# An SSD mixer in a two-block network: the state's share of the second chunk summed by TensorE, and the step sizes worked out earlier

## What is computed

```python
def mamba2_mixer(h, w_in, conv_w, conv_b, dt_bias, a_log, d_skip, norm_g, w_out):
    proj = h @ w_in                         # z (2048), xbc (3072), dt_raw (32)
    xbc = jax.nn.silu(causal_dwconv(xbc, conv_w, conv_b))
    dt = jax.nn.softplus((dt_raw + dt_bias).astype(jnp.float32))
    a = -jnp.exp(a_log.astype(jnp.float32))
    y = ssd_chunked(xs, dt, a, bm, cm) + xs * d_skip[:, None]
    yz = (y * jax.nn.silu(z))               # then an RMS norm in 4 groups, times norm_g
    return y @ w_out

def ssd_chunked(xs, dt, a, bm, cm):
    a_cs = jnp.cumsum(da, axis=-1)
    xdt = x * dtc[..., None]
    decay = jnp.exp(jnp.where(causal, a_cs[..., :, None] - a_cs[..., None, :], -jnp.inf))
    cb = jnp.einsum('bclgn,bcsgn->bcgls', cc, bc)
    y_diag = jnp.einsum('bcgrls,bcsgrp->bclgrp', cb[:, :, :, None] * decay, xdt)
    decay_states = jnp.exp(a_cs[..., -1:] - a_cs)
    states = jnp.einsum('bclgn,bcgrl,bclgrp->bcgrpn', bc, decay_states, xdt)
    y_off = jnp.einsum('bclgn,bcgrpn,bcgrl->bclgrp', cc, prev, jnp.exp(a_cs))
    return (y_diag + y_off)
```

## Times and profile before

| | |
|---|---|
| median of 3 runs | 1482.74 us (1481.03 to 1485.03) |
| the profiled execution | 1484.64 us |
| its span, first to last instruction | 1482.9 us |
| PE / PEld busy | 93% / 89% of the span |
| DVE / ACT / POOL busy | 70% / 51% / 10% |
| mean granted TensorE clock | 0.964 of 2.4 GHz |

### The profile page before, as it was taken

The page is one execution under the profiler, slowest core; times in us unless marked ns, Lnnn a source line. Parts: engine busy times, 40 slices in busy tenths (PEclk is TensorE's granted clock), DMA queues, the critical chain, the costliest instruction groups (busy, mean ns, idle before and its releaser), DMA issues.

```text
span 1482.9 us, 30231 instructions
## 1 busy us (share of the span) xinstructions
PE 1381.3 (93%) x12445; PEld 1325.4 (89%) x12445; DVE 1040.0 (70%) x1688; ACT 761.6 (51%) x1257; POOL 141.5 (10%) x147
## 2 busy tenths in 40 slices
PE   7998999997798999999997599999999998899997
PEld 6997988896798999999995499999999887899997
DVE  5769898986676656557696877887555655678843
ACT  5594483326645444354563855544454455554432
POOL 2000000000101111001002102211010100222100
PEclk9999999997999999999999699999999999999999
DMA  8533510210262665645445344554655521455550
GB/s 267 171 113 114 172 56 2 88 60 30 92 194 86 205 191 165 198 149 160 154 135 153 114 154 158 172 174 148 219 171 175 196 85 59 157 185 170 180 190 29
DMA packets 204338, 211.05 MB, mean 142 GB/s; under 512 B 8579, under 2 KB 201867, under 8 KB 204059
## 3 DMA queue, kind: packets, MB, share of 16 engines
q1 hardware_dynamic: 202154, 200.87, 42.7%
q0 software_dynamic: 1968, 8.44, 2.0%
q10 hardware_dynamic: 96, 0.02, 0.0%
HBM read 207.70 MB, written 1.62 MB: 141 GB/s over the span
## 4 chain that ended last, share of the span: by engine, by line
PE 71%; DVE 16%; ACT 5%; issue 4%; DMA 2%; POOL 1%; SPq 0%; DVEq 0%; ACTq 0%; POOLq 0%
PE pb L417 19%; PE pb L419 19%; PE pb L418 19%; DVE w_lo L446 2%; DVE pj L1453 2%; PE pb L1937 1%; DVE sub L1381 1%; PE pb L403 1%; PE pb L2307 1%; DVE x_lo L1229 1%; PE pb L1979 1%; PE pb L1926 1%; ACT w_hi L440 1%; DVE sub L1382 1%; PE pb L1932 1%
## 5 line engine op out<-in xcount | busy, mean ns | idle before, releaser
L446 DVE TENSOR_TENSOR w_lo<-raw,w_hi 128x1024 fp32r<-128x1024 f32 (+1 forms) x384 | 471.3, 1230 | 161.1 <-ACT w_hi L440 160.5
L417 PE MATMUL pb<-x_hi,w_hi 128*128 128x256 f32 x1968 | 564.2, 287 | 19.8 <-DVE w_lo L446 10.1
L440 ACT ACTIVATE w_hi<-raw 128x1024 fp32r<-128x1024 f32 (+1 forms) x384 | 395.5, 1042 | 340.9 <-PE pb L419 298.9
L418 PE MATMUL pb<-x_lo,w_hi 128*128 128x256 f32 x1968 | 559.9, 284 | 0.0
L419 PE MATMUL pb<-x_hi,w_lo 128*128 128x256 f32 x1968 | 559.8, 284 | 0.0
L417 PEld LDWEIGHTS pb<-x_hi,w_hi 128*128 128x128 f32 x1968 | 381.1, 194 | 24.7 <-DVE w_lo L446 15.9
L418 PEld LDWEIGHTS pb<-x_lo,w_hi 128*128 128x128 f32 x1968 | 381.0, 194 | 0.3
L419 PEld LDWEIGHTS pb<-x_hi,w_lo 128*128 128x128 f32 x1968 | 380.8, 193 | 0.0
L417 PE MATMUL pb<-act_hi,w_hi 128*128 128x256 f32 x528 | 149.5, 283 | 1.1 <-DVE w_lo L446 1.1
L418 PE MATMUL pb<-act_lo,w_hi 128*128 128x256 f32 x528 | 149.4, 283 | 0.0
L419 PE MATMUL pb<-act_hi,w_lo 128*128 128x256 f32 x528 | 149.4, 283 | 0.0
(11 more groups left out here) (312 smaller groups left out, 2103.2 us busy)
## 6 DMA issues: line engine op xcount, KB each, us to landing
raw<-in_ffn_w_up_dram SPq DMA_DIRECT2D x55, 1024.0 KB, 5.1
raw<-in_w_in_dram SPq DMA_DIRECT2D x28, 1024.0 KB, 5.1
raw<-in_ffn_w_down_dram SPq DMA_DIRECT2D x24, 896.0 KB, 4.8
raw<-in_ssd_w_in_dram SPq DMA_DIRECT2D x20, 1024.0 KB, 5.3
raw<-in_fox_w_in_dram SPq DMA_DIRECT2D x16, 1024.0 KB, 5.8
raw<-in_ffn_w_down_dram SPq DMA_DIRECT2D x12, 1024.0 KB, 5.3
raw<-in_ffn_w_gate_dram SPq DMA_DIRECT2D x11, 1024.0 KB, 5.3
raw<-in_ssd_w_out_dram SPq DMA_DIRECT2D x8, 1024.0 KB, 6.3
```

The costliest lines, as they stand in the source:

```text
L417: pe.matmul(o, w_hi[m][:, k, :], hi[:, k0 + k, :], start=first and k == 0, stop=False)
L418: pe.matmul(o, w_hi[m][:, k, :], lo[:, k0 + k, :], start=False, stop=False)
L440: act.activation(w_hi[m][:, 0:nk, :], raw[s][:, 0:nk, m * P:(m + 1) * P], ACT.Copy).then_inc(sem("w_hi_ready"), 1)
L446: dve.tensor_tensor(w_lo[m][:, 0:nk, :], raw[s][:, 0:nk, m * P:(m + 1) * P], w_hi[m][:, 0:nk, :].bitcast(F32), ALU.subtract).then_inc(sem( ...
```

## The change

- `ssd_dt` is no layer any more. Its weights `dt_w` (128 KB) are loaded by SP ahead of `down0`'s, after a wait for the last `w_lo` of `up0`; the 8 products stand between `ssd_z` and `ssd_xbc`.
- The step sizes are worked out inside `ssd_xbc`, after the second block of its first unit, on VectorE and ScalarE. ScalarE also takes exp(acs) of the second chunk (32 x 128), which goes through DRAM to `eab`; `eab` is now the second half of `y_ssd`, and nobody takes its exponential after the broadcast. All six decay pieces are issued then. VectorE's layer code for `ssd_xbc` is written out for two units (`lead=2`) before its loop.
- `xdt_end` is made by VectorE in four parts behind `xdt` 4 to 7, `b_tok` and `xdt_end` lie where `x_hi` and `x_lo` were.
- The state's part (`chunk_states`) stands behind the first four y instead of ahead of the loop.
- In the second chunk TensorE first multiplies the identity by the two tiles of `y_ssd` into the bank, and the four heads' products add to it; VectorE takes all pieces out with the same instruction as in the first chunk, and L1768 is gone. A `sync` on VectorE's own instructions stands in rounds 8 to 16. `w_lo` for `ssd_out` moves to rounds 9 to 11, its `w_hi` into the last unit of `ssd_xbc`.

```diff
+        x_hi_base = nc.sbuf_base
...
         xdt = pj[:, 56:72, :].rearrange("p a b -> p (a b)").rearrange("p (c f) -> p c f", c=2)
-        xdt_end = pj[:, 72:80, :].rearrange("p a b -> p (a b)")
-        NATT = 6
+        x_hi_plain = nc.alloc_sbuf_tensor_at("x_hi_plain", [P, KC * T], F32, offset=x_hi_base)
+        x_lo_plain = nc.alloc_sbuf_tensor_at("x_lo_plain", [P, KC * T], F32, offset=x_hi_base + KC * T * 4)
+        xdt_end = x_lo_plain[:, :]
+        NATT, FIRST_UNITS = 6, 4
...
         da_end = small[:, 0:P]
-        eab = sub[:, 0:8, :].rearrange("p a b -> p (a b)").rearrange("p (m l) -> p m l", l=P)
-        b_tok = x_gain[:, 0:2, :].rearrange("p a b -> p (a b)").rearrange("p (g n) -> p g n", g=SSD_GROUPS)
+        eab = y_ssd[:, :, P:T]
+        dt_w = pj[:, 90, :].rearrange("p (k n) -> p k n", n=SSD_HEADS)
+        acs_exp = small[:, P:T]
+        b_tok = x_hi_plain[:, 0:512].rearrange("p (g n) -> p g n", g=SSD_GROUPS)
...
-        layer("ssd_dt", narrow(a["ssd_w_in_2"][0], 5120, SSD_HEADS), [KC], dmas=(1, 0))
...
             units(act, ly, body, 2 if begin else lead)
...
-            units(dve, ly, body, 2 if begin else 0)
+            units(dve, ly, body, 2 if begin else lead)
...
+                if ly.name == "down0":
+                    sp.wait_ge(sem("w_lo_ready"), L["up0"].item1)
+                    sp.dma_start(dt_w, a["ssd_w_in_2"][0].rearrange("(k p) n -> p k n", p=P)[:, :, 5120:5120 + SSD_HEADS]).then_inc(sem("dt_w_loaded"), 16)
...
             pool.wait_ge(sem("acs_ready"), 2)
-            pool.dma_start(acs_dram.rearrange("c h l -> h c l"), acs.rearrange("h (c l) -> h c l", c=2)).then_inc(sem("sub_dma"), 16)
+            pool.dma_start(acs_dram[0:2].rearrange("c h l -> h c l"), acs.rearrange("h (c l) -> h c l", c=2)).then_inc(sem("sub_dma"), 16)
             pool.wait_ge(sem("sub_dma"), ACS_OUT)
-            pool.wait_ge(sem("xbc_ready"), SSD_XBC)
+            for i in range(NATT):
+                decay_piece(i)
+            pool.wait_ge(sem("da_ready"), 1)
+            pool.dma_start(acs_dram[2], acs_exp).then_inc(sem("sub_dma"), 16)
+            pool.wait_ge(sem("sub_dma"), ACS_OUT + 16)
             for h in range(2):
...
+                src = acs_dram[2].rearrange("(a m t) l -> t a m l", a=1, t=2)[h]
                 pool.dma_start(eab[64 * h:64 * h + 64, :, :], src.broadcast_to([64, SSD_Z, P])).then_inc(sem("sub_dma"), 16)
-            for i in range(2):
-                decay_piece(i)
-            pool.wait_ge(sem("xdt_ready"), 4)
-            pool.tensor_tensor(xdt_end.rearrange("p (h d) -> p h d", d=HEAD),
-                               xdt[:, 0, :].rearrange("p (h d) -> p h d", d=HEAD),
-                               tok_heads[:, 4, :].unsqueeze(2).broadcast_to([P, SSD_HEADS, HEAD]), ALU.mult).then_inc(sem("xdt_end_ready"), 1)
-            pool.wait_ge(sem("st_done"), SSD_GROUPS)
-            for i in range(2, 16):
-                if i >= NATT:
-                    pool.wait_ge(sem("y_done"), i - NATT + 1)
+            for i in range(NATT, 16):
+                pool.wait_ge(sem("y_done"), i - NATT + 1)
                 decay_piece(i)
...
+                if isinstance(u, int) and (u, m) == (0, 1):
+                    step_sizes()
+
+            def step_sizes():
+
+                log_exp()
+                act.wait_ge(sem("small_loaded"), 16 * 12)
+                go(act.activation(heads_col[:, 3:4], heads_col[:, 1:2], ACT.Exp))
+                act.wait_ge(sem("abs_ready"), 1)
+                link(act.activation(dt_e, dt_e, ACT.Exp, scale=-1.0))
+                act.activation(dt_e, dt_e, ACT.Ln, bias=1.0).then_inc(sem("log_ready"), 1)
+                act.wait_ge(sem("acs_ready"), 2)
+                act.activation(acs_exp, acs[:, P:T], ACT.Exp)
+                act.activation(da_end, acs[:, 0:P], ACT.Exp, scale=-1.0, bias=acs[:, P - 1:P]).then_inc(sem("da_ready"), 1)
...
-            act_layer(act, L["ssd_xbc"], xbc_hook, lead=2)
+            act_layer(act, L["ssd_xbc"], xbc_hook, lead=2, nxt=L["ssd_out"])
...
-            act.wait_ge(sem("abs_ready"), 1)
-            link(act.activation(dt_e, dt_e, ACT.Exp, scale=-1.0))
-            act.wait_ge(sem("small_loaded"), 16 * 12)
-            go(act.activation(heads_col[:, 3:4], heads_col[:, 1:2], ACT.Exp))
-            act.activation(dt_e, dt_e, ACT.Ln, bias=1.0).then_inc(sem("log_ready"), 1)
-            act.wait_ge(sem("acs_ready"), 2)
-            act.activation(da_end, acs[:, 0:P], ACT.Exp, scale=-1.0, bias=acs[:, P - 1:P]).then_inc(sem("da_ready"), 1)
-
-            DECAYS_IN = 48 + 32
-            act.wait_ge(sem("sub_dma"), DECAYS_IN)
-            for b in range(4):
-                t = eab[:, 4 * b:4 * b + 4, :]
-                act.activation(t, t, ACT.Exp).then_inc(sem("eab_ready"), 1)
-            ahead(act_head, act, L["ssd_out"])
-            act.wait_ge(sem("evac_done"), L["ssd_z"].evac1 + BANKS)
 
...
-                if i == 0:
-                    act.wait_ge(sem("eab_used"), 4)
+                if i == 10:
+                    act.wait_ge(sem("evac_done"), L["ssd_z"].evac1 + BANKS)
...
-            dve_layer(dve, ly, xbc_block, rest_last=True)
...
+            def step_sizes(u, m):
+
+                if not (isinstance(u, int) and (u, m) == (0, 1)):
+                    return
+                dve.wait_ge(sem("narrow_done"), 1)
+                dve.wait_ge(sem("small_loaded"), 16 * 12)
...
+            dve_layer(dve, ly, xbc_block, step_sizes, rest_last=True, lead=2)
+            dve.wait_ge(sem("heads_turned"), 1)
+            flat_heads = tok_heads[:, :, :].rearrange("p a h -> p (a h)")
+            link(dve.tensor_copy(flat_heads, pb[4][:, 0:5 * SSD_HEADS]))
+            dve.nop().then_inc(sem("heads_ready"), 1)
...
+                if i >= 4:
+                    dve.wait_ge(sem("xdt_ready"), b + 1)
+                    tt(xdt_end[:, 512 * b:512 * b + 512].rearrange("p (h d) -> p h d", d=HEAD),
+                       xdt[:, 0, 512 * b:512 * b + 512].rearrange("p (h d) -> p h d", d=HEAD),
+                       tok_heads[:, 4, 8 * b:8 * b + 8].unsqueeze(2).broadcast_to([P, 8, HEAD]), ALU.mult).then_inc(sem("xdt_end_ready"), 1)
...
+            def chunk_states():
+
+                for g in range(SSD_GROUPS):
+                    dve.wait_ge(sem("st_done"), g + 1)
+                    dve.tensor_copy(st_ssd[:, 512 * g:512 * g + 512], pb[6 + g % 2][:, :]).then_inc(sem("st_ready"), 1)
+
+                for b in range(4):
+                    dve.wait_ge(sem("yoff_done"), b + 1)
+                    dve.wait_ge(sem("sub_dma"), 96)
+                    tt(y_ssd[:, 4 * b:4 * b + 4, P:T], pb[4 + b % 2][:, :].rearrange("p (m l) -> p m l", l=P),
+                       eab[:, 4 * b:4 * b + 4, :], ALU.mult).then_inc(sem("eab_used"), 1)
+                dve.wait_ge(sem("eab_used"), 4)
+
             for i in range(17):
+                if i == FIRST_UNITS:
+                    chunk_states()
+                if i >= 8:
+                    sync()
                 if i < 16:
...
-                    if c == 0:
-                        for r in range(2):
-                            m = 2 * hq + r
-                            ins = stt(y_ssd[:, m, 0:P], xbc[:, m, 0:P], d_skip[:, m:m + 1], src[:, r, :], ALU.mult, ALU.add)
-                            if r == 0:
-                                go(ins)
-                        ins.then_inc(sem("y_out_ssd"), 1)
-                    else:
+                    for r in range(2):
+                        m = 2 * hq + r
+                        ins = stt(y_ssd[:, m, P * c:P * c + P], xbc[:, m, P * c:P * c + P], d_skip[:, m:m + 1], src[:, r, :], ALU.mult, ALU.add)
+                        if r == 0:
+                            go(ins)
+                    ins.then_inc(sem("y_out_ssd"), 1)
+                    if c == 1:
                         yy = y_ssd[:, 2 * hq:2 * hq + 2, :]
-                        tt(yy[:, :, P:T], yy[:, :, P:T], src, ALU.add).then_inc(sem("y_out_ssd"), 1)
-
+                        sync()
                         dve.wait_ge(sem("z_silu"), 4)
                         dve.wait_ge(sem("y_out_ssd"), i)
                         tt(yy, yy, z_t[:, 2 * hq:2 * hq + 2, :], ALU.mult).then_inc(sem("yz_ready"), 1)
-                if i < 8:
-                    for m in (2 * i, 2 * i + 1):
-                        go(stt(y_ssd[:, m, P:T], xbc[:, m, P:T], d_skip[:, m:m + 1], y_ssd[:, m, P:T], ALU.mult, ALU.add))
-                if i == 8:
-                    sync()
-                if 4 <= i < 4 + LOOKAHEAD:
-                    dve_rest(dve, L["ssd_out"], 0, 0, i - 4)
+                if 9 <= i < 9 + LOOKAHEAD:
+                    dve_rest(dve, L["ssd_out"], 0, 0, i - 9)
...
+            pe.wait_ge(sem("dt_w_loaded"), 16)
+            narrow_product(dt_w, SSD_HEADS, 1)
             pe_layer(pe, L["ssd_xbc"], x_hi, x_lo, "x_lo_ready", X_BASE[2])
-            s = L["ssd_dt"].u0 % 2
-            pe.wait_ge(sem(f"landed{s}0"), L["ssd_dt"].landed[0][0])
```

(21 more changed lines are left out.)

89 lines of the change are left out of this document (27 added, 62 removed).

## The result

The changed kernel took 1488.58 us (median of 20 runs, 1481.18 to 1497.07) against 1482.80 us of before (20 runs, 1477.00 to 1488.97). That is 5.8 us slower: the ratio is 1.0045, with a 95% interval of 1.0027 to 1.0063, or 4.0 to 9.3 us. The prediction said 1481.6 and a range up to 1488.0, so the median lies outside, and on the side that it gave 0.16.

The account below looks back on a forecast made before the run. TensorE was taken as the bound (71% of the chain), with single waits in the SSD mixer. Costs 3.6 + 2.5 + 1.3 less a gain of 8.5 made -1.1 us: 1481.6 us, range 1475.5 to 1488.

Parts of the forecast that it names:

- The dt product is no gain here.: Behind `ssd_xbc`: removing the product gains nothing, since scores wait for xbc's last Silu and start at 789.22 either way.
- the forecast +7.3: Checkpoint: the first `xdt` starts 7.3 us after the end of `ssd_xbc`, 2.8 us earlier than in the kernel before.
- The idle time of "some 3 us": TensorE, between the last `xs` turn at 798.2 and the first y at 801.5: idle some 3 us, against 4.2 before.
- the 10.7 us forecast: `chunk_states` behind four y: from 805.1 to 815.8, near the half-clock end; bounds 813.5 at full clock, 817.0 at half.
- The rounds: Attention loop on VectorE: 1.12 us a round in chunk 0, 3.05 in rounds 9 to 11; identity products hide beside VectorE.
- The tail behind multiply 12: End of the attention loop: multiply 12 to 15 takes 8.3 us, against 8.2 before.
- Step sizes in `ssd_xbc`, 2.5 us.: VectorE reaches later work in `ssd_xbc` 2.8 us late, 0.3 of it slack: cost 2.5 us, bounds 1.2 to 4.2.
- SP's wait, 1.3 us.: At `down0`, first weights queue behind dt_w's delayed load: first product at 593.9, not 592.65; cost 1.3 us, bounds 0.5 to 2.0.
- the three costs: Ahead of the end of `ssd_xbc`: dt product 3.6 us, step sizes 2.5, SP's wait at `down0` 1.3.
- the slower case: Rival: `ssd_xbc` falls behind as VectorE's `w_lo` comes late, +5.5 us, so +4.4 in all, 1487.2 us; chance 0.16.
- Full clock: Rival: four y units keep TensorE at 2.4 GHz through state products and group sums, -4.6 us in all, 1478.1; chance 0.20.
- The rule of the Trainium skill: Basis of a rival: transposes not counting as activity, half clock from the turns on, +0.1 us, 1482.8; chance 0.14.

Follow-up runs that it names:

- e3: Changed kernel plus seven unused products on TensorE ahead of the wait for xbc's last tiles, before the scores: median 1483.21 us, ratio 1.0019 to before.
- e5: Changed kernel without SP's wait at `down0`, dt product and step sizes in `ssd_z`, useless products ahead of scores and first attention block: 1475.96 us, ratio 0.9969 to before.
- e6: Changed kernel without the identity products; VectorE adds the sum and the `d_skip` multiply-adds return: 1490.25 us, ratio 1.0061 to before; SSD stage 240.4 us against 238.2.
- e10: Kernel of e5 without the identity products; VectorE adds again: 1482.44 us, ratio 1.0002 to before; SSD stage 233.6 us against 231.4.
- e4: Changed kernel with the dt product and step sizes moved into `ssd_z`: 1487.99 us, ratio 1.0038 to before; SSD stage 235.9 us.
- e1: Changed kernel without SP's wait ahead of the dt weights' load at `down0`: medians 1491.09 and 1492.07 us, ratios 1.0067 and 1.0065 to before.
- e2: Kernel before plus only SP's wait and the unused dt weights' load at `down0`: 1489.02 us, ratio 1.0039 to before.
- g1: Changed kernel without SP's wait at `down1`, plus six unused products in fox's 2.87 us wait: 1482.10 us, ratio 0.9985 to before.
- g2: Kernel before without SP's wait at `down1`, plus six unused products in fox's 2.87 us wait: 1476.80 us, ratio 0.9949 to before.
- e7: Changed kernel with the chunk states ahead of the loop, not behind four units: 1490.94 us, ratio 1.0066 to before; SSD stage 239.2 us.
- e11: Kernel before without SP's wait ahead of fox's narrow weights at `down1`: 1479.16 us, ratio 0.9981 to before.
- e8: Kernel before with only the dt product moved ahead of `ssd_xbc`, its weights loaded at `down0` without a wait: 1481.88 us, ratio 1.0007 to before.

## Why the prediction was wrong

The forecast was -1.1 us, and the first pair of profiles differs by +8.0. Of the 9.1 us between, 2.4 lie at `down0`, 3.0 in the SSD stage and 3.7 in stages without an edit. In the two touched stages the same step fails: an idle time of TensorE was priced as idle time alone, or at nothing, and the half clock behind it was left out. In the others the forecast put everything at nothing, and why their clock differs between the kernels stays open in part.

- *"The dt product is no gain here."* This is the step that failed first in the SSD stage. It was right that the scores start no sooner without the product, and wrong that nothing else hangs on it. The product kept TensorE's clock up: without it, 3.27 us idle, scores 3.79 for 2.05, the clock at 0.50 in 796 to 800. e3 puts useless products there and gets the first `xdt` at the forecast +7.3, and 1.7 us off the stage behind T'.
- *The idle time of "some 3 us" ahead of the first y* was seen, and half clock for `chunk_states` forecast. But the forecast took it as given; e5 shows that it is worth 3.1 us. The state part took the 10.7 us forecast; it ended at T' + 32.9 and not + 30.4 since it began 2.5 late, 1.9 of it from the loop's late start.
- *The rounds.* 1.12 us in chunk 0 and 3.07 in rounds 10 and 11 came as worked out (round 9 took 3.46), and the identity's products hide up to round 12 but for a wait of 0.28 us in round 9. The titled part is worth 2.2 us (e6, e10). The tail behind multiply 12 was 0.9 us longer than forecast up to multiply 15 (9.2 against 8.3): the group sums (3.33) stood at half clock still.
- *Step sizes in `ssd_xbc`, 2.5 us.* Measured 1.9; the mechanism was right, and e4 takes it away.
- *SP's wait, 1.3 us.* The wait was 1.9, near the upper bound of 2.0, and the bound was of the wait alone. What the clock loses behind it, 1.7 us, was in no term, though the earlier trace rows had shown the same thing behind another wait. 3.6 for 1.3: the largest miss of the three costs (e1, e2).
- *Everything else at nothing.* Up1 + down1 and fox, with no edit in them, were 2.1 to 3.6 and 3.9 to 5.8 us longer in all three profiles of the changed kernel. At `down1` TensorE waited 1.93 to 2.19 us, with half clock behind it, against 1.12 and 1.39 without; why the weights came later isn't shown. In fox the waits are equal and the clock isn't. g1 and g2 show that, with the waits at `down1` and in fox taken out in both kernels, 5.3 us are left between the medians, and 5.6 of the profiles' 7.4 us lie in the two touched stages.
- *The range.* Its lower end is 1476.0 and not 1475.5 by its own bounds (1478.1 - 1.3 - 0.8); nothing hangs on it.
- *The rivals.* None was what happened. The median is in the direction of the slower case, but not by its mechanism. Full clock did not come by itself; e5 shows what it needed. `ssd_xbc` fell behind by 1.9 us, not 5.5. The rule of the Trainium skill (TensorE: Matmul & The Clock Gate, "Part 4: PE-mode transpose") that turns do not count as activity finds no support here either: in the changed kernel the clock stayed at 1.00 in 802 to 806, when TensorE did nothing but turns, and in g2 it rose from 0.50 to 1.00 with nothing but turns run (the rows stand in the last section).

Open: why the medians of e1 (1491 and 1492 us) aren't below the changed kernel's though its stage is 3.6 us shorter; and what makes one wait cost clock and an equal one not. The profiles show only that a kernel repeats its own pattern.

## What to carry to other kernels

Price a wait of TensorE with the half clock behind it: waits of 1.9 us cost 3.6 here. Before moving "hidden" work off an engine that waits anyway, ask what clock the next products will have; if nothing useful can stand there, a few products into a free bank gave 1.7 and 3.1 us in the stage here. And cut both profiles at the same instruction into stages, touched and untouched, before explaining a difference: nearly half of this one (3.7 of 8.0 us) stood in code that nobody had changed.

## What the runs showed of the hardware that was not expected

- TensorE's waits at the first product of `down0` and `down1`, in all 20 profiles, those over 0.9 us. Behind nine of 1.12 to 1.71 us the clock stayed at 1.00. Behind 15 of 1.77 to 2.31 us it went to 0.50 for some 3 us, and only behind one, 1.79 us (e10), it did not.
- The wait behind the norm ahead of `up1` is 2.29 or 2.30 us in all 20. Half clock followed in 16, none in four (before's second profile, e7, e11, g2). So length alone does not decide, and a kernel that moves by some us can gain or lose at a place that it doesn't touch.
- Moving 3.6 us of TensorE's work ahead of the path changed the SSD stage of before by -0.6 or +0.9 us (e8 against its two profiles), since a DMA's round trip got 2.0 us shorter and the state products 2.8 or 1.5.
- Turns alone brought the clock back in g2. Its wait of 2.13 us ahead of the turns is the same as in before, but here half clock followed. TensorE did only turns from 793 to 801, at 0.50 for over 6 us and then at 1.00; behind `down0`'s wait, with ordinary products, half clock lasted some 3 us. TensorE's timeline and the stretches:

```profile
793.63 7.21 PE L1936 MATMUL pb<-ident,pj 128*128 128x128 f32 x32
```

```profile
793.00:799.00 6.00, 5.99 (x29) 4.92 (x29) 4.59 (x8) 0.00 (x0) 2.54 (x5) 0.50 0.58 171
800.00:801.00 1.00, 0.77 (x6) 0.42 (x4) 0.94 (x3) 0.00 (x0) 1.00 (x1) 1.00 1.02 217
```
